# Two-layer transformer in float32 on one core: where the mean of the layer norms is summed

## What is computed

```python
ALPHA = (2 * DEPTH) ** 0.25

def layer_norm(x, g, b):
    xf = x.astype(jnp.float32)
    mu = jnp.mean(xf, axis=-1, keepdims=True)
    var = jnp.mean(jnp.square(xf - mu), axis=-1, keepdims=True)
    y = (xf - mu) * lax.rsqrt(var + LN_EPS) * g.astype(jnp.float32) + b.astype(jnp.float32)
    return y.astype(x.dtype)

for l in range(DEPTH):
    h = hybrid_mixer(x, ...)
    x = layer_norm(ALPHA * x + h, ln1_g[l], ln1_b[l])
    h = memory_cross_attention(x, mem, x_wq[l], x_wkv[l], x_wo[l])
    x = layer_norm(ALPHA * x + h, ln2_g[l], ln2_b[l])
    h = conv_ffn(x, f_w_up[l], f_conv_k[l], f_conv_b[l], f_w_down[l])
    x = layer_norm(ALPHA * x + h, ln3_g[l], ln3_b[l])
x = second_block(x, ...)
```

## Time and profile before

| | us |
|---|---|
| Median of three runs | 4088.2 |
| Lowest and highest | 4087.5, 4094.07 |
| The profiled execution | 4084.68 |
| Its span in the trace | 4082.7 |
| PE busy in it | 3713.7 |
| DVE, ACT, POOL busy | 1538.7, 1003.1, 1851.1 |

### The profile page before, as it was taken

One profiled execution on the slowest core, in us unless ns is written; L12 is line 12 of the kernel. 1 busy time (PEld: TensorE's weight loads), 2 busy tenths in 40 slices (PEclk: granted clock), 3 DMA queues, 4 the chain that ended last, 5 costly groups with the idle time before them and its releaser, 6 DMA issues.

```text
span 4082.7 us, 45107 instructions
## 1 busy us (share of the span) xinstructions
PE 3713.7 (91%) x18221; PEld 2797.9 (69%) x18221; DVE 1538.7 (38%) x2312; ACT 1003.1 (25%) x1943; POOL 1851.1 (45%) x1218
## 2 busy tenths in 40 slices
PE   7999887999988998879999799998799889979998
PEld 5677665777756776657777476776688657657875
DVE  3454423424134554244241454333533143225341
ACT  1334113212023341232110454332210023211010
POOL 3343552555533444525555243433466533335663
PEclk8999999999999999999999799999899989989999
DMA  4121221655321213215553122221333222122332
GB/s 124 54 62 58 83 78 47 187 165 150 93 60 54 62 52 88 78 57 166 164 149 85 42 74 61 70 57 46 86 94 93 83 62 62 42 73 75 96 89 61
DMA packets 578694, 345.22 MB, mean 85 GB/s; under 512 B 15935, under 2 KB 561976, under 8 KB 578488
## 3 DMA queue, kind: packets, MB, share of 16 engines
q1 hardware_dynamic: 574541, 337.34, 28.7%
q10 hardware_dynamic: 3947, 4.99, 0.4%
HBM read 340.14 MB, written 2.14 MB: 84 GB/s over the span
## 4 chain that ended last, share of the span: by engine, by line
PE 83%; DVE 7%; ACT 6%; POOL 2%; issue 2%; DMA 0%; ACTq 0%; SPq 0%; POOLq 0%; DVEq 0%
PE gemm L216 22%; PE gemm L218 21%; PE gemm L217 21%; PE outs L297 8%; PE scores L297 5%; POOL w_low L203 1%; PE gemm L253 1%; PE scores L1405 1%; PE gemm L255 1%; PE gemm L254 1%; DVE work L1394 1%; ACT tiles L594 1%; ACT tiles L621 1%; POOL w_high L201 1%; DVE tiles L1498 0%
## 5 line engine op out<-in xcount | busy, mean ns | idle before, releaser
L201 POOL CAST w_high<-w_raw 128x1024 fp32r<-128x1024 f32 (+3 forms) x585 | 549.2, 939 | 2109.8 <-PE gemm L218 1737.6
L203 POOL TENSOR_TENSOR w_low<-w_raw,w_high 128x1024 fp32r<-128x1024 f32 (+3 forms) x585 | 1227.2, 2098 | 46.9
L216 PE MATMUL gemm<-x_high,w_high 128*128 128x512 f32 x2584 | 1050.8, 407 | 51.8 <-POOL w_low L203 39.1
L217 PE MATMUL gemm<-x_low,w_high 128*128 128x512 f32 x2584 | 1019.1, 394 | 0.0
L218 PE MATMUL gemm<-x_high,w_low 128*128 128x512 f32 x2584 | 1018.7, 394 | 0.0
L216 PEld LDWEIGHTS gemm<-x_high,w_high 128*128 128x128 f32 x2584 | 493.2, 191 | 207.7 <-issue 50.0
L216 PE MATMUL gemm<-split_tiles,w_high 128*128 128x512 f32 (+1 forms) x1456 | 580.1, 398 | 27.0 <-DVE split_tiles L531 9.5
L218 PEld LDWEIGHTS gemm<-x_high,w_low 128*128 128x128 f32 x2584 | 491.7, 190 | 108.6 <-issue 0.8
L217 PE MATMUL gemm<-split_tiles,w_high 128*128 128x512 f32 (+1 forms) x1456 | 565.3, 388 | 0.0
L218 PE MATMUL gemm<-split_tiles,w_low 128*128 128x512 f32 (+1 forms) x1456 | 564.6, 388 | 0.0
L217 PEld LDWEIGHTS gemm<-x_low,w_high 128*128 128x128 f32 x2584 | 493.0, 191 | 100.5 <-issue 4.0
(11 more groups left out here) (344 smaller groups left out, 3652.8 us busy)
## 6 DMA issues: line engine op xcount, KB each, us to landing
w_raw<-in_mod_w SPq DMA_DIRECT2D x96, 512.0 KB, 3.7
w_raw<-in_mlp_w SPq DMA_DIRECT2D x96, 512.0 KB, 4.0
w_raw<-in_w_in SPq DMA_DIRECT2D x88, 512.0 KB, 3.8
w_raw<-in_f_w_up SPq DMA_DIRECT2D x88, 512.0 KB, 4.9
w_raw<-in_e_w_in SPq DMA_DIRECT2D x48, 512.0 KB, 3.9
w_raw<-in_o_w_in SPq DMA_DIRECT2D x30, 512.0 KB, 3.9
w_raw<-in_w_branch SPq DMA_DIRECT2D x48, 256.0 KB, 2.7
w_raw<-in_mlp_w SPq DMA_DIRECT2D x32, 384.0 KB, 3.3
```

Source lines behind the costliest of these rows:

```text
L201: me.pool.tensor_copy(WH[:, h, 0:n], W32[:, s, 0:n]).then_inc(sem["pool_done"], 1)
L203: me.pool.tensor_tensor(WL[:, h, 0:n], W32[:, s, 0:n], WH[:, h, 0:n].bitcast(F32), ALU.subtract).then_inc(sem["w_split"], 1)
L216: me.pe.matmul(o, wh, hi, start=begin and k == 0, stop=False)
L217: me.pe.matmul(o, wh, lo, start=False, stop=False)
```

## The change

For j = 0 nothing happens any more. For each j from 1 to 7 DVE adds tile j to a running sum in tile 13 of `T` (for j = 1 tiles 0 and 1 are added), behind a wait on its own last addition to the residual. When j is 7, PE waits for that sum and makes one matmul with the constant matrix. PE waits for no residual tile otherwise. Lines below `mean_part` move by 4.

```diff
         def mean_part(me, j, added):
 
-            if me.pe and j >= 1:
-                mm(me, O[:, 0, :], M["mean"], X[:, j - 1, :], j == 1, False)
+            total = T[:, 13, :]
+            if j > 0:
+                summed = me.tick("dve_step")
+                if me.dve:
+                    me.dve.wait_ge(sem["dve_step"], added)
+                    me.dve.tensor_tensor(total, X[:, 0, :] if j == 1 else total, X[:, j, :],
+                                         ALU.add).then_inc(sem["dve_step"], 1)
             if j == KD - 1:
                 me.mean_made = me.tick("pe_step")
-            if me.pe:
-                me.pe.wait_ge(sem["dve_step"], added)
-                if j == KD - 1:
-                    mm(me, O[:, 0, :], M["mean"], X[:, j, :], False, True).then_inc(sem["pe_step"], 1)
+                if me.pe:
+                    me.pe.wait_ge(sem["dve_step"], summed)
+                    mm(me, O[:, 0, :], M["mean"], total).then_inc(sem["pe_step"], 1)
```

## The result

The changed kernel takes 4052.7 us (median of 6 runs, 4050.0 to 4055.8) beside 4087.9 us before; the ratio is 0.9912, with a 95% interval of 0.9899 to 0.9925. The forecast was 4050 us and a range of 4044 to 4061. Two later sets of runs, each with its own runs of the kernel before, gave 0.9913 (0.9901 to 0.9926) and 0.9915 (0.9901 to 0.9929). So the gain is 35 us where 38 were forecast; the interval is 31 to 41 us, and by the runs alone the two can't be told apart. The profiled execution took 4053.1 us with a span of 4051.1 us, 31.6 us less than the profiled one of before.

A forecast was written before the change was run, and what follows sets the result against it. PE was taken to bound the kernel (busy 91% of the span). From the 4088.2 us median, -44.2 us at boundaries and +6.0 for last sums gave -38.2, so 4050 us, range 4044 to 4061.

The forecast's parts named there:

- The boundaries, 44.2 us: Between a product's units, last to second matmul falls to 0.45 us: 7.36 us saved per norm, 44.2 for six.
- The last sum, 1.0 us each: At each product's end the mean waits for DVE's last addition, held up by POOL's cast: 1.0 us later, 6.0 in all.
- loses the port twice: Rival: at product ends POOL's subtraction also gets ahead of the last addition, 3.5 us later each; 4065 us, chance 0.07.
- `x_wo`, 0 to 4 us: At 14 boundaries in `x_wo`, POOL's later weight splits could hold PE up to 0.3 us each; taken as zero.
- The clock, 12 us at 0.08: Rival: PE's idling before the mean brings one more low-clock stretch per norm, 2 us each; 4062 us, chance 0.08.
- 38.2: Net gain forecast for six norms: 44.2 us saved at boundaries less 6.0 us added by the last sums.

The follow-up runs named there:

- without the sum: Changed kernel with no running sum; its one mean matmul takes residual tile 7 alone, so the result is wrong: 4041.8 us, ratio 0.9888 to before.
- The waits alone: Kernel before, keeping its mean matmuls, but PE waits for residual tile j-1 ahead of its matmul, not tile j behind it: 4074.0 us, ratio 0.9967.
- the last tile for itself: Changed kernel with the running sum over tiles 0 to 6 only and tile 7 multiplied separately by PE: 4046.9 and 4045.2 us, ratios 0.9898 and 0.9896.

## Why the prediction was right, point by point

- **The boundaries, 44.2 us.** Measured 44.3 without the sum. The number was right and the reading behind it was not. I wrote that in the earlier trace rows PE waits for nothing and the mean costs its full length, and so put a matmul behind units 1 to 6 and a wait behind unit 0. The wait for DVE's addition ended last at all seven; the mean was hidden in it. The total came out right because it took the whole boundary, from the last matmul ahead to the second behind, compared it with one that has neither, and the change takes both away. A forecast for one of the two alone, by the same reading, would have been wrong, as my expectation for the waits was.
- **The last sum, 1.0 us each.** As forecast from the earlier trace rows at four of the six ends, down to the 0.54 us behind the cast's end, and the experiment with an operand in PSUM shows the cause. At the two ends of `x_wo` I had the wrong instruction: I took POOL's place from the slower kernel of before, and POOL was late there, still in the subtraction ahead of the cast. As little of it was left, that cost 0.85 us and not more. The rival that it loses the port twice did not occur in any of the three traces.
- **`x_wo`, 0 to 4 us.** The splits got later by 0.48 us and not 0.32, and PE waited for them at six of the 14 boundaries; 0.13 us each, 0.8 us in all. Near the end that I took, and it makes up for what the two ends lack: 5.7 + 0.8 = 6.5 us where 6.0 were added, right in the total by luck, and a little off in both parts.
- **The clock, 12 us at 0.08.** Low clock between the products did grow, from 73 and 83 us to 96, 96 and 120, about the 24 us that this rival put on it. Its cause, the pause, is not shown, since the variants in which PE goes straight into the mean have as much. Its price was wrong: I charged half of the time at low clock, as if PE were streaming in it, and 14 us more of it in one stretch cost nothing. No steady loss is shown but the 1.6 us behind `x_wo` 0, which the pause doesn't cause.
- **38.2 against 35 us.** The products hold 37.8 of it in each trace. The first trace of before, from which the sum was made, lies at the lower end of what the kernel does (4084.7 where its medians are 4088 to 4091), and single executions of either kernel stray by 5 us or more. The 1.6 us would account for half of what is short; the rest isn't told from that scatter, and 38.2 lies inside the interval of the runs. So there may be nothing missing at all.

## What to carry to other kernels

Where a matmul and a wait stand at the same boundary, compare the waited-for instruction's end with the next start before pricing either: here both had to go. The waits alone were worth 2 us a product, and the matmuls alone next to nothing, to judge by the boundary that had none. A reduction that moves to VectorE should leave out the last tile: sum what is early, and let the matmul engine take the last one for itself, so that nothing is added behind the last result. If the last sum must be waited for, keep one operand in PSUM while GpSimd works on SBUF.

## What was not expected of the hardware

- Two float32 matmul instructions of 512 columns are recorded as 1.02 us of busy PE, but the record of the next matmul can start 0.45 us behind theirs (513.00 after 512.55), so a wait of some 0.2 us leaves no idle time in the trace.
- A DVE addition of two SBUF tiles delays POOL by more than I had read: the low parts in `x_wo` took 1.77 us instead of 1.29, and the cast behind the last sum 1.50 instead of 1.04.
- Behind `f_w_down` of layer 0, in a window of 31 us, the mean granted clock was 0.72 in both traces of before and 0.61 in the three of the changed kernel, and two spare matmuls in PE's pause of 1.8 us restored 0.72; yet the variant without the sum (a pause of 0.78 us) and one trace with the last tile for itself (none) had 0.61 too. The kernel's time hardly followed.
- The same program lost 6.3 us to low clock behind one norm in one execution and nothing there in two others.
